# A mixture of experts scattered four experts at a time, and two norms whose small steps move to ScalarE

## The reference

```python
def layer_norm(x, g, b):
    mu = mean(x, -1); var = mean(square(x - mu), -1)
    return (x - mu) * rsqrt(var + EPS) * g + b

def grouped_moe(x, router_w, router_b, w_gate, w_up, w_down):
    gates = route_gates(x, router_w, router_b)   # top-1 group of 4, top-2 experts in it; zero elsewhere
    out = 0
    for e in range(16):
        h = silu(x @ w_gate[e]) * (x @ w_up[e])      # (256, 1024) @ (1024, 256)
        out = out + gates[:, e:e+1] * (h @ w_down[e])  # (256, 256) @ (256, 1024)
    return out
```

## Time and profile before

| | |
|---|---|
| median of 3 runs | 722.87 us (722.4 to 724.38) |
| profiled execution, its own time | 723.68 us |
| its span, first to last instruction | 721.8 us |
| PE / PEld busy | 697.4 us (97%) / 560.4 us (78%) |
| DVE / ACT / POOL busy | 408.0 (57%) / 280.5 (39%) / 48.3 us (7%) |
| DMA | 176.10 MB, mean 244 GB/s |

### The profile page before, as it was taken

The page is one execution under the profiler, slowest core; times in us unless marked ns, Lnnn a source line. Parts: engine busy times, 40 slices in busy tenths (PEclk is TensorE's granted clock), DMA queues, the critical chain, the costliest instruction groups (busy, mean ns, idle before and its releaser), DMA issues.

```text
span 721.8 us, 11939 instructions
## 1 busy us (share of the span) xinstructions
PE 697.4 (97%) x4744; PEld 560.4 (78%) x4744; DVE 408.0 (57%) x724; ACT 280.5 (39%) x471; POOL 48.3 (7%) x93
## 2 busy tenths in 40 slices
PE   7999999999999999999799999999999999999992
PEld 7989987889988875656399798888898897655551
DVE  4885886674575752111477588848646567212126
ACT  3545643355543331111424466435455252311111
POOL 1720000010041000000011000001000010000000
PEclk9999999999999999999989999999999999999997
DMA  8991334574358499999985313445633685999961
GB/s 283 332 366 57 113 126 171 186 238 153 118 189 343 191 382 400 414 417 414 359 298 168 127 59 118 157 164 194 239 124 110 239 349 222 355 420 417 415 269 61
DMA packets 62702, 176.10 MB, mean 244 GB/s; under 512 B 3872, under 2 KB 37104, under 8 KB 53424
## 3 DMA queue, kind: packets, MB, share of 16 engines
q1 hardware_dynamic: 58112, 161.69, 60.2%
q0 software_dynamic: 4096, 12.25, 5.1%
q10 hardware_dynamic: 432, 1.31, 0.5%
HBM read 174.19 MB, written 1.05 MB: 243 GB/s over the span
## 4 chain that ended last, share of the span: by engine, by line
PE 60%; issue 31%; DVE 3%; POOL 2%; DMA 1%; ACT 1%; DVEq 1%; POOLq 0%; ACTq 0%
PE ring L2122 8%; PE ring L1688 7%; PE ring L1689 7%; PE ring L1690 7%; PE ring L2157 4%; PE quad L1688 4%; PE quad L1689 4%; PE quad L1690 4%; PE quad L2169 2%; PE ring L1730 2%; PE ring L1856 1%; PE ring L1759 1%; DMA X<-in_x 1%; PE ring L1749 1%; PE ring L1954 1%
## 5 line engine op out<-in xcount | busy, mean ns | idle before, releaser
L1004 DVE TENSOR_TENSOR w_lo<-raw,w_hi 128x1024 fp32r<-128x1024 f32 x108 | 127.7, 1222 | 39.0 <-ACT w_hi L691 33.9
L691 ACT CAST w_hi<-raw 128x1024 fp32r<-128x1024 f32 x108 | 108.0, 1049 | 65.1 <-PE quad L1690 60.3
L1688 PE MATMUL ring<-x_hi,w_hi 128*128 128x256 f32 x320 | 92.9, 290 | 0.8 <-ACTq L734 0.7
L1689 PE MATMUL ring<-x_lo,w_hi 128*128 128x256 f32 x320 | 90.5, 283 | 0.0
L1690 PE MATMUL ring<-x_hi,w_lo 128*128 128x256 f32 x320 | 90.5, 283 | 0.0
L714 ACT ACTIVATE arena<-ring 128x512 f32<-128x512 f32 (+1 forms) x66 | 35.5, 573 | 84.7 <-PE ring L1690 65.1
L1597 DVE TENSOR_TENSOR y_lo<-ring,y_hi 128x512 fp32r<-128x512 f32 x32 | 22.1, 692 | 72.9 <-ACT y_hi L958 72.9
L1688 PEld LDWEIGHTS ring<-x_hi,w_hi 128*128 128x128 f32 x320 | 61.3, 192 | 2.3 <-issue 1.9
L1689 PEld LDWEIGHTS ring<-x_lo,w_hi 128*128 128x128 f32 x320 | 61.3, 192 | 0.7 <-issue 0.5
L1690 PEld LDWEIGHTS ring<-x_hi,w_lo 128*128 128x128 f32 x320 | 61.3, 192 | 0.0
L2122 PE MATMUL ring<-raw,x_slots 128*64 128x256 f32 x448 | 51.3, 380 | 0.0
(11 more groups left out here) (322 smaller groups left out, 1421.5 us busy)
## 6 DMA issues: line engine op xcount, KB each, us to landing
raw<-in_moe_w_gate SPq DMA_DIRECT2D x20, 1024.0 KB, 7.0
w_raw<-in_moe_w_down SPq DMA_DIRECT2D x18, 1024.0 KB, 10.9
raw<-in_moe_w_up SPq DMA_DIRECT2D x16, 1024.0 KB, 7.7
raw<-in_w_in SPq DMA_DIRECT2D x14, 1024.0 KB, 11.3
raw<-in_moe_w_down SPq DMA_DIRECT2D x12, 1024.0 KB, 10.1
raw<-in_w_out SPq DMA_DIRECT2D x10, 1024.0 KB, 5.1
raw<-in_xattn_wk SPq DMA_DIRECT2D x8, 1024.0 KB, 5.9
raw<-in_xattn_wv SPq DMA_DIRECT2D x8, 1024.0 KB, 4.8
```

What stands on the lines that cost most here:

```text
L691: nc.scalar.copy(unit_slot(u, 0, n)[:, s], raw[:, SLOT[u], s]).then_inc(hi_done, 1)
L1004: low = nc.vector.tensor_tensor(unit_slot(u, 1, n)[:, s], raw[:, SLOT[u], s], unit_slot(u, 0, n)[:, s].bitcast(F32), ALU.subtract)
L1688: mm(out, a_hi, b_hi, start=first, stop=False)
L1689: mm(out, a_hi, b_lo, start=False, stop=False)
```

## The change

1. **Fours.** `to_slot` keeps only the 32 slots that each tile can fill: 16 x 32 = 512 columns a tile. Four experts together then fill 128 slots of a tile, so that gates of slots, turns and scatter go over 4 fours instead of 8 pairs. The down projection still goes by pairs. Its output rows of (tile, expert) must be sorted into a four's rows, so `out_high` and `out_low` move each half in four pieces of 32 partitions (`quarters`), each from a start partition to another. `slot_gates` is made by 8 small reductions instead of 4 operations. In the loop, odd j run scatter, turn and down; even j run half of the down projection, the turn, and the other half. Behind the last down comes one scatter.
2. **Third norm.** Both tiles' statistics are ScalarE's; `lv` (variance + EPS) is made there too, not on GpSimd. The first pass of the norm waits for the mean alone and writes to `off_mean`. The next layer's `x_high` comes ahead of `hi_rotary`, and `keep_busy` gets 3 and 2 instead of 6 and 3 rounds.
3. **Second norm.** `shift` is made by ScalarE right before it is used.

```diff
-SCALAR_TILE = {0: 1, 2: 0}
-BY_SCALAR = sorted(SCALAR_TILE)
-BY_VECTOR = [(i, t) for i in range(3) for t in range(T) if SCALAR_TILE.get(i) != t]
-def stats_made(l, i):
-    return l * len(BY_SCALAR) + BY_SCALAR.index(i) + 1
+SCALAR_TILES = {0: (1,), 1: (), 2: (0, 1)}
+BY_SCALAR = [(i, t) for i in range(3) for t in SCALAR_TILES[i]]
+BY_VECTOR = [(i, t) for i in range(3) for t in range(T) if t not in SCALAR_TILES[i]]
+def stats_made(l, i, t):
+    return l * len(BY_SCALAR) + BY_SCALAR.index((i, t)) + 1
...
+off_mean = at(1024, T, D)
...
-to_token = rounded("to_token", 6000, PAIRS, SEQ)
+to_token = rounded("to_token", 6000, FOURS, SEQ)
...
-return (y_hi, y_lo)[t][:, 4:8, :].rearrange("p a b -> p (a b)")
+return (y_hi, y_lo)[t][:, 4:6, :].rearrange("p a b -> p (a b)")
...
+def quarters(j):
+    for t in range(T):
+        for i in range(2):
+            q = 2 * (j % 2) + i
+            yield t, slice(32 * q, 32 * q + 32), slice(64 * i + 32 * t, 64 * i + 32 * t + 32)
...
 def ln_power(i):
     for t in range(T):
-        if SCALAR_TILE.get(i) != t:
+        if t in SCALAR_TILES[i]:
+            pool.wait_ge(ln_stats, stats_made(l, i, t))
+        else:
             pool.wait_ge(ln_var, var_made(l, i, t))
-        else:
-            pool.wait_ge(ln_stats, stats_made(l, i))
-            nc.gpsimd.tensor_scalar(lv[:, t:t + 1], about_mean[:], 1.0 / D, EPS, ALU.mult, ALU.add)
-            pool.drain()
         nc.gpsimd.tensor_tensor(lr[:, t:t + 1], lv[:, t:t + 1], minus_half[:, 0:1],
                                 ALU.pow).then_inc(ln_rstd, 1)
-        if i == 1:
-            pool.drain()
-            nc.gpsimd.tensor_tensor(shift[:, t:t + 1], neg_mean[:, t:t + 1], lr[:, t:t + 1],
-                                    ALU.mult).then_inc(shift_ready, 1)
...
+for t in SCALAR_TILES[n]:
+    act.wait_ge(ln_sum, stats_made(l, n, t))
+    nc.scalar.activation(passed, X[:, t, :], ACT.Copy, scale=-1.0 / D, accum_out=minus_mean[:, t:t + 1])
+    act.drain().then_inc(mean_ready, 1)
+    nc.scalar.activation(passed, X[:, t, :], ACT.Square, bias=minus_mean[:, t:t + 1],
+                         accum_out=about_mean[:, t:t + 1])
+    act.drain()
+    nc.scalar.activation(lv[:, t:t + 1], about_mean[:, t:t + 1], ACT.Copy, bias=EPS,
+                         scale=1.0 / D).then_inc(ln_stats, 1)
...
-act.wait_ge(shift_ready, l * T + t + 1)
+act.wait_ge(ln_rstd, l * (3 * T) + (T + t + 1))
+nc.scalar.activation(shift[:, t:t + 1], neg_mean[:, t:t + 1], ACT.Copy, scale=lr[:, t:t + 1])
+act.drain().then_inc(shift_ready, 1)
...
 norm_stats(2, l)
 if l + 1 < DEPTH:
+    x_high("xa", l + 1)
     hi_rotary(l + 1)
-    x_high("xa", l + 1)
 else:
...
-nc.scalar.copy(y_of(y_hi, j, a),
-               out_bank(j, a).rearrange("p (a b) -> p a b", a=2)).then_inc(out_hi, 1)
+for t, to, rows in quarters(j):
+    nc.scalar.copy(y_of(y_hi, t, a)[to],
+                   out_bank(j, a)[rows].rearrange("p (a b) -> p a b", a=2)).then_inc(out_hi, 1)
...
-for b in range(4):
+for b in range(2):
...
 def norm_affine(n, l, t):
+    source = X[:, t, :]
+    if t in SCALAR_TILES[n]:
+        dve.wait_ge(mean_ready, stats_made(l, n, t))
+    if n < 2:
+        dve.wait_ge(ln_rstd, l * (3 * T) + (n * T + t + 1))
+    else:
+        source = off_mean[:, t, :]
+    by_scalar = t in SCALAR_TILES[n]
+    mean, op = (minus_mean[:, t:t + 1], ALU.add) if by_scalar else (mv[:, t, 0:1], ALU.subtract)
+    nc.vector.scalar_tensor_tensor(source, X[:, t, :], mean, ln_w[:, 0, :], op, ALU.mult).then_inc(ln_read, 1)
+    dve.drain()
     dve.wait_ge(ln_rstd, l * (3 * T) + (n * T + t + 1))
-    by_scalar = SCALAR_TILE.get(n) == t
-    mean, op = (minus_mean[:], ALU.add) if by_scalar else (mv[:, t, 0:1], ALU.subtract)
-    nc.vector.scalar_tensor_tensor(X[:, t, :], X[:, t, :], mean, ln_w[:, 0, :], op, ALU.mult).then_inc(ln_read, 1)
-    dve.drain()
     if n == 2 and l + 1 == DEPTH and t == 1:
         for s in (slice(0, D // 2), slice(D // 2, D)):
-            last = nc.vector.scalar_tensor_tensor(X[:, t, s], X[:, t, s], lr[:, t:t + 1], ln_w[:, 1, s],
+            last = nc.vector.scalar_tensor_tensor(X[:, t, s], source[:, s], lr[:, t:t + 1], ln_w[:, 1, s],
                                                   ALU.mult, ALU.add)
             if s.start == 0:
                 last.then_inc(half_normed, 1)
     else:
-        nc.vector.scalar_tensor_tensor(X[:, t, :], X[:, t, :], lr[:, t:t + 1], ln_w[:, 1, :],
+        nc.vector.scalar_tensor_tensor(X[:, t, :], source, lr[:, t:t + 1], ln_w[:, 1, :],
                                        ALU.mult, ALU.add).then_inc(ln_read, 1)
     dve.drain().then_inc(x_ready, 1)
...
-norm_stats(1)
+dve.sem_inc(ln_sum, 1)
...
-nc.vector.tensor_tensor(to_slot(t)[:, 512 * half:512 * half + 512].rearrange("p (e s) -> p e s", e=E // 2),
-                        view(slots[:, t, :], [[0, E // 2], [1, EXPERT_SLOTS]]),
-                        view(mine, [[1, E // 2], [0, EXPERT_SLOTS]]), ALU.is_equal).then_inc(slots_ready, 1)
+nc.vector.tensor_tensor(to_slot(t)[:, SEQ * half:SEQ * half + SEQ].rearrange("p (e s) -> p e s", e=E // 2),
+                        view(slots[:], [[0, E // 2], [1, TILE_SLOTS]]),
+                        view(mine, [[1, E // 2], [0, TILE_SLOTS]]), ALU.is_equal).then_inc(slots_ready, 1)
...
 def out_low(j):
     for a in range(2):
-        dve.wait_ge(out_hi, l * 2 * PAIRS + (2 * j + a + 1))
-        last = nc.vector.tensor_tensor(y_of(y_lo, j, a),
-                                       out_bank(j, a).rearrange("p (a b) -> p a b", a=2),
-                                       y_of(y_hi, j, a).bitcast(F32), ALU.subtract)
-        last.then_inc(out_split, 1)
+        for n, (t, to, rows) in enumerate(quarters(j)):
+            dve.wait_ge(out_hi, l * 8 * PAIRS + (8 * j + 4 * a + n + 1))
+            nc.vector.tensor_tensor(y_of(y_lo, t, a)[to],
+                                    out_bank(j, a)[rows].rearrange("p (a b) -> p a b", a=2),
+                                    y_of(y_hi, t, a)[to].bitcast(F32), ALU.subtract).then_inc(out_split, 1)
...
-for e in range(2):
-    rows = of_pair(e)
-    parts = ring[rows, 3, 0:2 * E].rearrange("p (j e) -> p e j", e=4)
-    nc.vector.tensor_copy(slot_gates[rows, :], parts[:, e, :])
-dve.drain()
-for e in range(2):
-    rows = of_pair(e)
-    parts = ring[rows, 3, 0:2 * E].rearrange("p (j e) -> p e j", e=4)
-    nc.vector.tensor_tensor(slot_gates[rows, :], parts[:, 2 + e, :], slot_gates[rows, :], ALU.add)
+for j in range(2):
+    for t, q, rows in quarters(j):
+        parts = ring[q, 3, 0:4 * E].rearrange("p (k t h e) -> p k t h e", k=FOURS, t=T, h=2)
+        nc.vector.tensor_reduce(slot_gates[rows, :].rearrange("p (k j) -> p k j", j=2)[:, :, j],
+                                parts[:, :, t, :, q.start // 32], AX_X, ALU.add)
...
-keep_busy(f"{name}3", l, (6, 3)[t])
+keep_busy(f"{name}3", l, (3, 2)[t])
...
-for j in range(PAIRS):
+for k in range(FOURS):
     for t in range(T):
-        r = mm(ring[:, 3, 4 * j:4 * j + 4], to_slot(t)[:, j * P:(j + 1) * P],
-               half_gates[:, t, j, :], start=t == 0, stop=t == T - 1)
+        at_col = 8 * (2 * k + t)
+        r = mm(ring[:, 3, at_col:at_col + 8], to_slot(t)[:, k * P:(k + 1) * P], half_gates[:, t, k, :],
+               start=True, stop=True)
 r.then_inc(slot_gated, 1)
...
 def to_token_turns():
-    for j in range(PAIRS):
+    for k in range(FOURS):
         for t in range(T):
-            c = (j % 2) * SEQ + t * P
-            r = nc.tensor.transpose(quad[:, j // 2, c:c + P],
-                                    to_slot(t)[:, j * P:(j + 1) * P].bitcast(F32), ident[:])
+            c = (k % 2) * SEQ + t * P
+            r = nc.tensor.transpose(quad[:, k // 2, c:c + P],
+                                    to_slot(t)[:, k * P:(k + 1) * P].bitcast(F32), ident[:])
     r.then_inc(to_token_done, 1)
...
-def down(j):
-    pe.wait_ge(turned_moved, l * PAIRS + (j + 1))
-    if 0 < j < PAIRS - 1:
-        pe.wait_ge(out_split, l * 2 * PAIRS + 2 * j)
+def down(j, halves=range(2)):
+    if 0 in halves:
+        pe.wait_ge(turned_moved, l * PAIRS + (j + 1))
+        if 0 < j < PAIRS - 1:
+            pe.wait_ge(out_split, l * 8 * PAIRS + 8 * j)
     w = [v.rearrange("p (c n) -> p c n", c=2)
          for v in pair_wait((down_unit(2 * j), down_unit(2 * j + 1)))]
-    for a in range(2):
+    for a in halves:
         for c in range(2):
             for i in range(2):
                 r = mm(out_bank(j, a)[of_pair(i), :], h_t[:, j % 2, c * P:(c + 1) * P][:, of_pair(i)],
                        w[i][:, c, 512 * a:512 * a + 512], start=c == 0, stop=c == 1)
-        if a == 0:
-            r.then_inc(half_out, 1)
-    r.then_inc(unit_used, 2)
-def scatter(j, tiles=range(T)):
+        r.then_inc(*((unit_used, 2) if a else (half_out, 1)))
+def scatter(k, tiles=range(T)):
     for t in tiles:
         for a in range(2):
-            pe.wait_ge(out_split, l * 2 * PAIRS + (2 * j + a + 1))
```

(64 more changed lines are left out.)

## The result

The changed kernel takes **724.43 us** (median of 20 runs, 723.01 to 725.68) against 722.85 us for the kernel before (20 runs): ratio 1.0018, 95% interval [1.0011, 1.0025]. The forecast was 717.4 us and the range 713 to 721.5. Nothing was gained; the 1.6 us lost lie inside the 0.3% that I had called no change. The profiled execution took 725.57 us, 1.1 above its median; its span is 723.7, 1.9 longer than before.

The account below looks back on a forecast made before the run. The weight stream was taken to set the end of the expert stage, TensorE leading by about 2 us. Layer 0: -2.05 - 3.05 + 1.85 + 0.2; layer 1: -2.15 - 2.1 + 1.85; together -5.45, so 717.4 us, range 713 to 721.5.

Parts of the forecast that it names:

- What starts the stream earlier: TensorE savings ahead of the load of 272.85 move all later weight landings: -3.05 us in layer 0, -2.1 in layer 1.
- rival 3: Expert weight stream doesn't follow the earlier start: +5.15 us, 722.5, no change; chance 0.10.
- the 1.8 us a layer of gates and turns: Gates of slots and turns, 8 instead of 16 instructions each: -0.9 -0.9 = -1.8 us a layer, moving the stream earlier.
- What I had reckoned ahead of gate(0): Second norm and gather: one-hots ahead of the gather -0.3 us a layer; shift on ScalarE -1.1 in layer 0, 0 in layer 1.
- The lead: TensorE's lead over the last down weights: of 5.9 us saved scatter a layer only -2.05 and -2.15 us count.
- The quarters and the end of the stage: Behind the last down: quarter splits 0.705 us apart on VectorE, 0.60 on ScalarE; third norm ends +1.85 us later a layer.
- TensorE behind the stage: Behind layer 0's experts, turns of x for tile 1 may run at the lower clock: +0.2 us.
- Rival 4: Waits for weights in the loop, 3.8 us a layer, let TensorE's clock fall: 719.5 to 722.5 us; chance 0.12.
- 1: Rival: quarters overlap as ordinary operations do, 0.60 us a split: -8.75 us, 714.1; chance 0.14, other better outcomes included.
- 2: Rival: TensorE, not the stream, ends the expert loop, so all 5.9 us count: 3.8 a layer more, 709.9; chance 0.04.
- 5: Rival: ScalarE and VectorE hinder each other in one PSUM bank: 726.8 us at 1.0 a split, 735.8 at 1.28; chance 0.08.

Follow-up runs that it names:

- half loads: Half the bytes of each expert's matrix loaded and used twice: on the kernel before 722.66 us, on the changed kernel 715.16 us.
- early_gate: The changed kernel with 5 fewer rounds of keep_busy ahead of the gather in each layer: 724.03 us.
- late_gate: The changed kernel with 12 more rounds of keep_busy ahead of the gather, and so ahead of gate(0), in each layer: 731.83 us.
- late_turns: The changed kernel with 12 more useless matmuls between gate(1) and the turns of the one-hot, behind the restart of the stream: 728.70 us.

## Why the prediction was wrong

**The step that failed is "What starts the stream earlier"**: it took -3.05 and -2.1 us, the landings moved by -0.5 us in layer 0 and, against gate(0), by +0.6 in layer 1. That is 5.2 of the 7.35 us between -5.45 and +1.9, and it is my rival 3, to which I gave 0.10. Inside this step it is the 1.8 us a layer of gates and turns, behind the restart, that failed: from gate(0) to the last landing it takes 0.4 us more than before in layer 0 and 0.6 more in layer 1.

What TensorE saves behind the restart does free places earlier (the load of 272.85 is issued at 270.20), as I reckoned. I took it that the stream had room for it there: it could deliver its eight units "no faster than 8 x 2.53 us, and it was a little slower than that". From the landing of the first load behind the restart to that of the load in question it takes 23.2 us before (255.0 to 278.2) and 23.6 after (254.1 to 277.7), where 8 x 2.53 is 20.2. The three missing microseconds stayed when the loads were issued 2.65 us earlier, so in the changed kernel a shortage of issued loads is not their cause. (In the kernel before it can have had a part: that load is issued 1.3 us ahead of its forerunner's landing, and the first load behind the restart, with nothing ahead of it, needs 4.8.) The DMA view from 259 to 279 us shows it (packets, MB, share of the engines' time), first of the kernel before:

```profile
q1 hardware_dynamic: 1370, 7.25, 91.8%
```

The same view of the changed kernel:

```profile
q1 hardware_dynamic: 1368, 7.46, 99.6%
```

The engines are fuller by 8 points and carry 3% more: the packets took longer. In both kernels the same four loads of layer 0 (down 3, up 6, down 4, down 7) land 2.9 to 4.2 us behind their forerunners, the others 2.4 to 2.8. In layer 1 the long ones are in part others, up to 4.7 us before and 4.1 after; there the change's eleventh load behind the restart still lands 1.0 us earlier against it than before, and one late long landing (680.5 us, 4.1 us behind its forerunner, before 2.55) takes more than that back. I had read the 0.91 of this window as starvation; the test would have been the landings one by one. From restart to last landing the ten profiled kernels with full loads take 95.9 to 98.1 us in layer 0 and 96.6 to 98.3 in layer 1, with no clear order by how early TensorE frees the places. With 4.8 us for the first load and 2.52 for each of the other 35 it would be 93.0 (an estimate from the short landings); the 3 to 5 us above it lie almost wholly in a few late landings. Why these are late stays open.

What I had reckoned ahead of gate(0) came true. GpSimd's first power of the second norm, which no edit changes, starts here in the kernel before, in the changed one and in the kernel before with half loads:

```profile
222.72 0.56 POOL L638 TENSOR_TENSOR lr<-lv,minus_half 128x1 f32<-128x1 f32 x1 [15.92 <-DVE lv L1088]
223.32 0.56 POOL L645 TENSOR_TENSOR lr<-lv,minus_half 128x1 f32<-128x1 f32 x1 [15.92 <-DVE lv L1097]
221.62 0.56 POOL L638 TENSOR_TENSOR lr<-lv,minus_half 128x1 f32<-128x1 f32 x1 [15.90 <-DVE lv L1088]
```

From there to gate(0) it takes 23.75 us before and 22.2 after in layer 0, 1.6 less for the 1.4 forecast (the wait of 1.1 us at line 1749 is gone, and no wait took its place), and 22.6 and 22.2 in layer 1, 0.4 less for 0.3 (which lies ahead of gate(0), though the table's forecasts have it in the third row). That gate(0) moved by only 0.95 us in the span is due to what lies ahead of the power, where the change's profile is 0.6 us late; the third line shows a profile 1.1 us early there with the same code up to there as the first, so a profile's absolute times in layer 0 are no better than about 1 us. And the 1.8 us of gates and turns lie behind the restart, so they count for nothing here.

**The lead** was cashed nearly as forecast: from the last landing to D it was 2.0 and 2.2 us before and is 0.13 after in both layers, so 1.85 and 2.05 us for 2.05 and 2.15. The half loads agree: with them D follows gate(0) another 6 us sooner in the changed kernel, and no sooner in the kernel before.

**The quarters and the end of the stage** had the right mechanism. Their steps were 0.60 and 0.718 us for 0.60 and 0.705; the adds came at D + 9.7 for D + 9.5. From there the estimate was short: x ready at D + 19.1 for D + 18.5. ScalarE ends tile 1's statistics at D + 16.6 (forecast 16.35), and from there over GpSimd's power to the last pass it takes 1.2 us, where I had put 0.7. The Trainium skill ("VectorE: DVE Perf Modes", section "Two Vector instructions with no wait between them") says of VectorE that an instruction that starts in another group of 32 partitions is held until the earlier ones have finished; the alternation of 0.71 and 0.61 agrees with it.

**TensorE behind the stage** was mis-sized: +0.2 us in layer 0 forecast, +0.8 measured. Layer 1's first unit starts at D + 22.8 instead of D + 19.65 (368.87), 3.2 us later, of which x ready explains 2.4. Waiting for quarters, TensorE runs its last scatter matmuls 0.43 us apart (0.25 at the full clock), idles 4.78 us and then has 1.2 GHz from 361.4 to 368.2 us, a stretch that holds nearly all turns of x. Rival 4 did not happen in the loop: the waits for weights there, up to 1.4 us each in layer 0 and once 2.4 us in layer 1, did not lower the clock once (1.00 from 250 to 347 us and from 600 to 702 us). The longest, in the waits of TensorE from 598 to 702 us:

```profile
PE ring L2170 <- DMA raw<-in_moe_w_down: 2.4, 1, 2.4
```

The Trainium skill ("TensorE: Matmul & The Clock Gate", section "HAM oscillation — how this bites in real kernels") says that waits for DMA inside a loop of matmuls lower the clock again and again; its example has waits of some 3 to 5 us, and no run here has waits that long in the loop. In layer 0 the clock fell at 354.55 us, behind a wait of 1.8 us and in one of 2.1 us for splits, with little work between them.

**Rivals.** 1 is excluded by the steps; 2 by the waits for weights; 5 by the steps too: with two engines in one bank a split lasts 0.69 us and starts 0.72 behind the last. (VectorE is always at least a quarter behind ScalarE, so the two read different partitions of the bank; the same ones at once were not tried.) 3 is what happened, and as the tail then stood without its counterweight the sum came out above zero. I had costed rival 3 at 722.5 with the tail as forecast; with the tails as measured (1.85 us more in all) it is 724.35. That this meets 724.43 to 0.1 us is luck: gate(0) to D alone differs by 0.7 us between the profiles of the change and of early_gate.

## What to carry to other kernels

Where engine work is removed beside a stream that is already full, count only the stream's lead; here any further gain needed an earlier start of the stream or fewer bytes. Whether a window with a share of 0.91 is starved or slow is read from its landings one by one. An edit that trades work in a covered loop for work at its end must be tried with the end left as it was: the same idea that loses 3.75 us over the whole stage gains 2.0 when the last two pairs are left out of it. And parts that were made together are to be timed apart: the norm edits alone were worth 3.6 us. Two profiles are compared from a mark just ahead of the changed code, not from the start of the span.

## What the runs showed of the hardware

- ScalarE behaves like VectorE: 32 x 512 copies start 0.60 us apart where the start partition changes and 0.484 where it stays. On VectorE it is about 0.71 and 0.61.
- In the first 30 us of the changed kernel's expert stage in layer 0 the weight stream delivers 377 GB/s at a share of 1.00, later 413 at 1.02. Instruction fetches of 16 KB (about 1 us each) lie at 259, 275 and 294 us, within 4 us ahead of three of the long landings, but the one at 310 us is followed by none and the long landing of up 6 at 271 us has none; whether they are the cause stays open.
- TensorE's clock comes back at different times behind layer 0's experts from kernel to kernel (0.82, 0.76 and 0.70 from 347 to 375 us in the change, late_gate and late_turns). From D to layer 1's gate(0) the latter two take 1.25 us (the added rounds left out) and 1.65 us more than the change; that the clock is the whole cause is not shown.
- Waits for weights of up to 2.4 us inside the loop left the granted clock at 1.00 (the changed kernel, layer 1).
